# Opening of the first layer: four blocks per channel group, every modulation sum on VectorE, and a new order of transfers

## What is computed

```
mod = dot(silu(c), w_ada) + b_ada
shift, scale, gate = split(mod, 3)
u = rms_norm(x, norm_w) * (1.0 + scale) + shift
proj = dot(u, w_in)
(fq, fk, fv, ff, fg, dq, dk, dv, iq, ik, iw, dg, sz, sxbc, sdt, mg) = split(proj, split_points)
```

## Time and profile before

| | |
|---|---|
| median of three runs | 3430.95 us (3424.48 to 3431.2) |
| the profiled execution | 3426.33 us, its span 3424.5 us |
| mean granted TensorE clock | 0.986 of full speed |
| TensorE busy | 3300.5 us, 96% of the span |
| VectorE busy | 2245.1 us, 66% |
| ScalarE busy | 1699.9 us, 50% |
| GpSimd busy | 46.8 us, 1% |
| transfers | 719.31 MB, mean 210 GB/s |

### The profile page before, as it was taken

The page is one execution under the profiler, slowest core; times in us unless marked ns, Lnnn a source line. Parts: engine busy times, 40 slices in busy tenths (PEclk is TensorE's granted clock), DMA queues, the critical chain, the costliest instruction groups (busy, mean ns, idle before and its releaser), DMA issues.

```text
span 3424.5 us, 43659 instructions
## 1 busy us (share of the span) xinstructions
PE 3300.5 (96%) x18122; PEld 2865.5 (84%) x18122; DVE 2245.1 (66%) x2695; ACT 1699.9 (50%) x2096; POOL 46.8 (1%) x90
## 2 busy tenths in 40 slices
PE   4899999999999999999999999999999999999998
PEld 3689979788888887898898878888898899988887
DVE  6778877866666556786666576655567776544454
ACT  4355664654443445556646544444447865434343
POOL 0000000000000000000000000000000000000000
PEclk8899999999999999999999999999999999999999
DMA  9754566567777555444444567765555443465553
GB/s 376 286 213 174 187 240 255 210 239 267 261 266 296 204 196 184 172 159 169 172 179 160 175 244 272 271 234 197 186 185 192 178 172 134 163 221 192 190 190 140
DMA packets 102917, 719.31 MB, mean 210 GB/s; under 512 B 12176, under 2 KB 12256, under 8 KB 18752
## 3 DMA queue, kind: packets, MB, share of 16 engines
q1 hardware_dynamic: 93888, 675.38, 53.6%
q0 software_dynamic: 8256, 37.64, 3.1%
q10 hardware_dynamic: 576, 3.50, 0.3%
HBM read 710.08 MB, written 6.40 MB: 209 GB/s over the span
## 4 chain that ended last, share of the span: by engine, by line
PE 87%; DVE 8%; ACT 3%; issue 1%; DMA 1%; DVEq 0%; ACTq 0%
PE G L1258 80%; DVE LL L1862 3%; PE BA L1406 1%; PE BD L1379 1%; PE BD L1441 1%; DVE S L2070 1%; DVE RAW L1873 1%; DMA KV<-in_x_dram 0%; ACT HH L1501 0%; PE BC L1392 0%; DVE RAW L1855 0%; DMA RAW<-in_w_ada_packed_dram 0%; PE BE L1324 0%; PE BA L1460 0%; PE BC L1460 0%
## 5 line engine op out<-in xcount | busy, mean ns | idle before, releaser
L1501 ACT ACTIVATE HH<-RAW 128x2048 fp32r<-128x2048 f32 x546 | 1044.8, 1914 | 1091.5 <-PE G L1258 1063.9
L1862 DVE TENSOR_TENSOR LL<-RAW,HH 128x2048 fp32r<-128x2048 f32 x546 | 1247.7, 2287 | 357.0 <-ACT HH L1501 356.6
L1258 PE MATMUL G<-HH,UH 128*128 128x512 f32 x2528 | 1005.7, 398 | 45.4 <-DVE LL L1862 40.5
L1258 PE MATMUL G<-LL,UH 128*128 128x512 f32 x2528 | 989.4, 391 | 0.0
L1258 PE MATMUL G<-HH,UL 128*128 128x512 f32 x2528 | 989.1, 391 | 0.0
L1258 PE MATMUL G<-UH,HH 128*128 128x256 f32 x2080 | 603.7, 290 | 11.6 <-DVE XS L2106 7.7
L1258 PEld LDWEIGHTS G<-HH,UH 128*128 128x128 f32 x2528 | 477.8, 189 | 149.8 <-DVE LL L1862 47.4
L1258 PE MATMUL G<-UH,LL 128*128 128x256 f32 x2080 | 589.7, 283 | 0.0
L1258 PE MATMUL G<-UL,HH 128*128 128x256 f32 x2080 | 589.6, 283 | 0.0
L1258 PEld LDWEIGHTS G<-LL,UH 128*128 128x128 f32 x2528 | 477.3, 189 | 101.4
L1258 PEld LDWEIGHTS G<-HH,UL 128*128 128x128 f32 x2528 | 477.9, 189 | 99.2 <-issue 2.6
(11 more groups left out here) (360 smaller groups left out, 2309.4 us busy)
## 6 DMA issues: line engine op xcount, KB each, us to landing
RAW<-in_w_in_packed_dram SPq DMA_DIRECT2D x402, 1024.0 KB, 4.8
RAW<-w_ada_turned_packed_dram SPq DMA_DIRECT2D x92, 1024.0 KB, 4.9
RAW<-in_w_out_packed_dram SPq DMA_DIRECT2D x48, 1024.0 KB, 4.8
RAW<-in_w_o_ssd_packed_dram SPq DMA_DIRECT2D x32, 1024.0 KB, 4.8
RAW<-in_w_o_fox_packed_dram SPq DMA_DIRECT2D x16, 1024.0 KB, 4.8
RAW<-in_w_o_dsa_packed_dram SPq DMA_DIRECT2D x16, 1024.0 KB, 4.8
RAW<-in_w_proj_a_packed_dram SPq DMA_DIRECT2D x16, 1024.0 KB, 4.8
RAW<-in_w_proj_b_packed_dram SPq DMA_DIRECT2D x16, 1024.0 KB, 4.8
```

The costliest lines, as they stand in the source:

```text
L1258: mm = pe.matmul(to, lt, rh, start=first, stop=end, skip_group_check=True)
L1501: a.activation(HH[g % NH][:, :n], RAW[buf(ch["f"])][:, :n], ACT.Copy).then_inc(*hi_done.up(g))
L1862: v.tensor_tensor(LL[buf(f)][:, :n], RAW[buf(f)][:, :n], HH[g % NH][:, :n].bitcast(F32), ALU.subtract).then_inc(*lo_done.up(g))
```

## The change

All eight dots of a group are made on VectorE, and the TensorE version of a dot with its banks, its semaphore and its addition in `am_first` is gone. A fourth block, the first half of `dq`, begins in `open` with the others, so there are four chunks per group; it sums in banks BD and BE. The transfers get an order of their own: eight dots, then a chunk behind every second dot, and the last three chunks at the end. Dots use five buffers (6, 7, 8, 0, 1), chunks four (2 to 5). The products are emitted one at a time, behind the first, third, fifth and seventh dot of the next group, each `lo` right before its product and the next chunk's `hi` after it. The four blocks' heads are turned into the banks of their own block and no longer into BE and BD, and these blocks no longer give their banks free early (`free_by`). `ada_maybe` uses what was already fetched, also where nothing new is to be fetched. In the plan, `dq` after `misc` is one block (four chunks) in place of two.

```diff
-DOT_BUFS, CHUNK_BUFS = [6, 7, 8, 0], [1, 2, 3, 4, 5]
+DOT_BUFS, CHUNK_BUFS = [6, 7, 8, 0, 1], [2, 3, 4, 5]
...
-        b = {"n": n, "set": n if n < 3 else (n - 3) % 2, "x": x, "ready": ready, "kts": kts, "evac": evac, "chunks": chunks,
+        b = {"n": n, "set": n if n < 4 else n % 2, "x": x, "ready": ready, "kts": kts, "evac": evac, "chunks": chunks,
...
-        if a["every"] and a["i"] < len(a["list"]):
+        if a["got"]:
+            self.ada_chunk()
+        if a["every"]:
             a["count"] += 1
-            if a["got"]:
-                self.ada_chunk()
             if a["next"] < len(a["list"]) and a["count"] * a["every"][0] % a["every"][1] < a["every"][0]:
                 self.ada_fetch()
...
     def open(self, blocks, between, am, u):
...
+        def dot(gi, i):
+            return "scale" if i < 4 else "shift", 4 * gi + i % 4
+
+        parts = [b["chunks"][gi] for gi in range(4) for b in blocks]
...
+        for n in range(32):
+            kind, ct = dot(*divmod(n, 8))
+            src = ("w_ada_turned", 0, (D if kind == "scale" else 0) + ct * P, P, [(0, D)])
+            self.dots[kind, ct] = self.fetch(src, ("dot_dve", kind, ct))
+            if n >= 7 and n % 2:
+                bring()
+        while len(self.chunks) < len(parts):
+            bring()
+
+        def multiply(g):
+            self.put("lo", g)
+            if g % 4 < 3:
+                self.put("hi", g + 1)
+            self.gemm(parts[g])
+            self.slot()
 
         for gi in range(4):
-            dots = [("scale", m, "dve") for m in range(4)] + [("shift", m, "dve") for m in range(4 - ON_PE)]
-            for m in range(4 - ON_PE, 4):
-                dots.insert(6, ("shift", m, "pe"))
-            for i, (kind, m, engine) in enumerate(dots):
-                if 4 <= i < 7:
-                    self.bring(chunk(gi, i - 4))
-                self.dot(kind, 4 * gi + m, engine)
+            for i in range(8):
+                self.put("dot_dve", *dot(gi, i))
                 between(gi, i)
-                if gi and i == 1:
+                if gi and i == 0:
                     u(gi - 1)
-                    multiply(gi - 1, (0, 1))
-                elif gi and i == 3:
-                    multiply(gi - 1, (2,))
+                if gi and i % 2 == 0:
+                    multiply(4 * gi - 4 + i // 2)
+            self.put("hi", 4 * gi)
             am(gi)
         u(3)
-        for n in range(2):
-            self.put("lo", chunk(3, n)["g"])
-        self.gemm(chunk(3, 0))
+        for g in (12, 13):
+            self.put("lo", g)
+            self.put("hi", g + 1)
+        self.gemm(parts[12])
         self.slot()
-        self.pend += [chunk(3, 1), chunk(3, 2)]
+        self.put("lo", 14)
+        self.put("hi", 15)
+        self.gemm(parts[13])
+        self.slot()
+        self.pend += parts[14:]
...
-            o.blocks[b]["free_by"] = ("hd_scaled" if HEADS[h[0]][0] else "hd_copied", h, 1)
...
-            o.open(iq_b + [dkv_b], first_x, am_first, u_first)
+            dq_b = [o.wblock(w, DQ, heads(("dq", 0, 0), True), u_ready, kind="tm", begun=True)]
+            o.open(iq_b + [dkv_b] + dq_b, first_x, am_first, u_first)
...
-        dq_b = [o.wblock(w, DQ + j * 512, heads(("dq", l, j)), u_ready, kind="tm") for j in range(2)]
+            dq_b = [o.wblock(w, DQ, heads(("dq", l, 0)), u_ready, kind="tm")]
+        dq_b.append(o.wblock(w, DQ + 512, heads(("dq", l, 1)), u_ready, kind="tm"))
...
-    GB.append([BA, BC])
+    GB += [[BA, BC], [BD, BE]]
...
     def turn_bank(h, t):
-        return BD if t and h in o.two_banks else BE
+        return GB[o.blocks[o.head_block[h]]["set"]][t] if h in o.own_banks else BE
...
         def am_first(gi):
...
-            v.wait_ge(*dot_pe.at("shift", c + 3))
-            v.tensor_tensor(SH[:, e:c + 4], pe_part[:, e - c:4], MOD[:, e:c + 4], ALU.add).then_inc(*own.up())
+            v.tensor_tensor(SH[:, c:c + 4], DOT[:, 0, c:c + 4], MOD[:, c:c + 4], ALU.add).then_inc(*own.up())
```

More of the change, by code:

```diff
@@ L31 @@
 NR, NX, NH = 6, 3, 3
-ON_PE = 1
-DOT_BUFS, CHUNK_BUFS = [6, 7, 8, 0], [1, 2, 3, 4, 5]
+DOT_BUFS, CHUNK_BUFS = [6, 7, 8, 0, 1], [2, 3, 4, 5]
 HEADS = {"iq": (None, "idx", 4), "dk": ("dsa", "rot", 2), "dq": ("dsa", "rot", 4), "fq": ("fox", None, 4),
@@ L115, in __init__ @@
         self.packed = {}
-        dots = list(DOT_BUFS)
-        self.ring, self.buf_user = {"dot_dve": dots, "dot_pe": dots, "all": list(CHUNK_BUFS)}, {}
+        self.ring, self.buf_user = {"dot_dve": list(DOT_BUFS), "all": list(CHUNK_BUFS)}, {}
         self.fetches = []
@@ L124, in __init__ @@
         self.evac_before, self.side_before = {}, {}
-        self.user = [None, None, None]
+        self.user = [None] * 4
         self.ada = {"list": [], "i": 0, "job": None, "every": 0, "count": 0, "next": 0, "got": []}
@@ L308, in ada_all, with bring @@
         self.until(a["job"])
[L310 to L317, removed]
-    def open(self, blocks, between, am, u):
[L323 to L330, removed]
-        for gi in range(4):
-            dots = [("scale", m, "dve") for m in range(4)] + [("shift", m, "dve") for m in range(4 - ON_PE)]
-            for m in range(4 - ON_PE, 4):
-                dots.insert(6, ("shift", m, "pe"))
-            for i, (kind, m, engine) in enumerate(dots):
-                if 4 <= i < 7:
-                    self.bring(chunk(gi, i - 4))
-                self.dot(kind, 4 * gi + m, engine)
+    def open(self, blocks, between, am, u):
+        def dot(gi, i):
+            return "scale" if i < 4 else "shift", 4 * gi + i % 4
+        parts = [b["chunks"][gi] for gi in range(4) for b in blocks]
+        def bring():
+            ch = parts[len(self.chunks)]
+            ch["g"] = len(self.chunks)
+            self.chunks.append(ch)
+            ch["f"] = self.fetch(ch["src"], ("gemm_done", ch["g"]))
+        for n in range(32):
[12 more added lines that the diff above has]
+            self.slot()
+        for gi in range(4):
+            for i in range(8):
+                self.put("dot_dve", *dot(gi, i))
@@ L378, in rope, with heads @@
         side_ended("rope_sin", r, 1)
-    def heads(h, two_banks=False):
+    def heads(h, own_banks=False):
         def at_once(b):
             o.head_block[h] = b
-            o.two_banks.add(h)
+            o.own_banks.add(h)
             for t in range(2):
                 put("hd", h, t)
-            o.blocks[b]["free_by"] = ("hd_scaled" if HEADS[h[0]][0] else "hd_copied", h, 1)
             yield
@@ L392, in steps @@
         def steps(b):
-            if two_banks:
+            if own_banks:
                 yield from at_once(b)
@@ L557, in out_layer @@
                 o.evac.add(modulated(l + 1))
-    o.head_block, o.tok_block, o.freed, o.two_banks = {}, {}, {}, set()
+    o.head_block, o.tok_block, o.freed, o.own_banks = {}, {}, {}, set()
     def load_layer(which):
@@ L982, in hybrid_stack @@
     ld_fk = count("ld_fk", o.all("fk_load"), 16)
-    dot_pe, dot_dve = count("dot_pe", o.all("dot_pe")), count("dot_dve", o.all("dot_dve"))
+    dot_dve = count("dot_dve", o.all("dot_dve"))
     ld_cb, cb_tanh, cb_silu = count("ld_cb", [()], 16), count("cb_tanh", [()]), count("cb_silu", [()])
@@ L1265, in begin @@
             pe.wait_ge(*ld_cst.at())
[L1267 to L1276, removed]
         def gate_cols(l):
@@ L1321, in hd_turn @@
             pe.wait_ge(*(hd_rot if rot else hd_scaled).at(h, t))
-            pe.wait_ge(*(hd_put.at(h, 0) if t and h not in o.two_banks else evac_before("hd", h, 0)))
+            pe.wait_ge(*(hd_put.at(h, 0) if t and h not in o.own_banks else evac_before("hd", h, 0)))
             for c in range(n):
@@ L1462, in lru_pe @@
             mm.then_inc(*lru_mm.up(ct))
-        todo = {"gemm": gemm, "start": begin, "dot_pe": dot, "gate_cols": gate_cols, "x_in": x_in, "xn_pe": xn_pe,
+        todo = {"gemm": gemm, "start": begin, "gate_cols": gate_cols, "x_in": x_in, "xn_pe": xn_pe,
                 "m_turn": m_turn, "hd_turn": hd_turn, "misc_pe": misc_mm,
@@ L1942, in am_first @@
             c = 4 * gi
-            e = c + 4 - ON_PE
-            pe_part = (BD, BE)[gi % 2]
             v.wait_ge(*ld_mod.at())
             v.wait_ge(*ld_par[0].at())
-            v.wait_ge(*dot_dve.at("shift", e - 1))
+            v.wait_ge(*dot_dve.at("shift", c + 3))
             v.tensor_tensor(AM[:, c:c + 4], DOT[:, 0, 16 + c:20 + c], MOD[:, 16 + c:20 + c], ALU.add).then_inc(*own.up())
-            v.tensor_tensor(SH[:, c:e], DOT[:, 0, c:e], MOD[:, c:e], ALU.add).then_inc(*own.up())
-            v.wait_ge(*dot_pe.at("shift", c + 3))
-            v.tensor_tensor(SH[:, e:c + 4], pe_part[:, e - c:4], MOD[:, e:c + 4], ALU.add).then_inc(*own.up())
+            v.tensor_tensor(SH[:, c:c + 4], DOT[:, 0, c:c + 4], MOD[:, c:c + 4], ALU.add).then_inc(*own.up())
             v.wait_ge(*own.last())
```

## The result

The changed kernel takes 3412.66 us (median of five runs, 3411.43 to 3414.68), the kernel before 3430.76 us (median of five, 3424.48 to 3431.2): the ratio is 0.9953, with a 95% interval of 0.9939 to 0.9967. The forecast was 3403 us, with a range of 3394 to 3421. So the direction is right and the time lies in the range, but the profiled executions differ by only 3426.33 - 3413.68 = 12.65 us, where the sum of the prediction said 24.2. About half of the sum was lost again. The kernel before has executions of 3424 to 3428 us and others of 3430 to 3432 (31 and 19 of its 50), and its profile (3426.33) is of the first kind, which is why the profiles differ by less than the medians.

The account below looks back on a forecast made before the run. The prediction took the length of a group's loop to bound the opening, and TensorE everything after. 10.8 + 16.4 - 3 = 24.2 us off the profiled 3426.3 gave 3402, forecast as a median of 3403 us, range 3394 to 3421.

Parts of the forecast that it names:

- Term one: Opening: the last group's first product starts at 135.6 instead of 146.4 us, a gain of 10.8 us.
- the first rival: Opening: transfers keep today's share of 0.94, 2.65 us each, 6 us later; 3409 us, chance 0.12.
- Term two: Behind the opening: TensorE has three chunks less to do, at 5.48 us each, a gain of 16.4 us.
- Term three: Convolution: side work behind `misc` starts later and its heaviest steps meet convolution steps, a cost of 3 us.
- The clock: Opening: slow clock after idle time between single chunks, 8.0 us per chunk after a fall; counted as costing nothing.
- The third rival: Opening: TensorE stays at 1.2 GHz throughout, 10.2 us per chunk, ending at 169; about 3434 us, chance 0.07.
- The second rival: Convolution: side work's delay costs some 15 us, 0.6 in each of 24 chunks; 3415 us, chance 0.14.
- The fourth: Before 350 us: VectorE bounds the stretch and the gain is given back; no change, 3429 us, chance 0.07.

Follow-up runs that it names:

- the best kernel: Changed kernel with two steps of side work instead of one behind four chunks at the end of the convolution: 3407.26 us, ratio 0.9941.
- the early catching up: Changed kernel with the four missing side steps taken behind chunks 45, 48, 51 and 53: 3411.05 us, ratio 0.9953.

## Why the prediction was half right

**Term one, the opening: right.** 9.45 us for 10.8. Cycle, start and end were as worked out. The 1.3 us that are missing are a start 0.3 later, a cadence of 2.51 us for each transfer instead of 2.49, and what is left behind the last dots. VectorE keeps up, no buffer is asked for late (the experiment with other buffers changes nothing), and the first rival (0.94 share) is refuted by the windows. What made the gain is less the removal of TensorE's dots, to which the prediction gave its first place: it alone gives 5.7 of the 17.4 us that the opening gives with three blocks. That the rest is the new order is argued by elimination: other buffers make no difference, pairs of products 2.7 us, and no run has the new order alone.

**Term two, three chunks less: right.** 15.9 us for 16.4.

**Term three: this is the step that failed, in size and in place.** The prediction put it at 3 us, at the meeting of `misc`'s side work and the convolution. That meeting costs no more than it said, 1.6 us of idle time and clock by the end of the convolution: TensorE's waits from 140 to 350 us on `LL`, first row of the list of waits of the changed kernel,

```profile
PE G L1265 <- DVE LL L1858: 4.4, 6, 1.7
```

were 2.6 without the one of 6.6 at 146.4. Idle time by 400 us is 2.4 us more than before. But the prediction followed the late lane only to the end of the convolution. The lane stays late for some 70 chunks, and where it meets the evacuation of the `sz` blocks, full steps of the attention stand in place of empty ones. From chunk 89 to 92 that is 5.2 us, the largest single piece. The whole term measures 12.6 us where the sum has 3. From 400 to 760 us there are 4.0 us more idle (15.8 against 11.8), and the granted clock was at 0.50 for 6.8 us between 640 and 760 before, for 17.1 after. Both experiments on the lane bear this out: making the old kernel's lane late costs it 9.1 us, clear of the noise, and catching up gives back 6.7 us of the changed one's profiled span (5.4 in the medians, 4.1 in the ratios, which is within the intervals). How much of the 12.6 the lateness causes isn't measured to the microsecond. The lateness is four chunks, not the five of the prediction.

**The clock: counted as nothing, and rightly so in the opening.** The third rival (1.2 GHz throughout) did not come: 0.95 to 1.00 from 60 to 120 us. By the section HAM oscillation of the Trainium skill (TensorE: Matmul & The Clock Gate), tiles shorter than the wait for their data go back to the slow clock one after the other; here the chunks of 5.5 us were longer than the 0.9 to 3.5 us between them, and the trace shows no fall at every chunk, only one of 3.4 us between 60 and 120 us, behind an idle stretch of 3.48 us at 73.5. Such a fall costs nothing there, as the prediction argued: with other buffers the clock fell twice for 6.8 us, and the last group started at 136.96 all the same. But the term was not nothing later: 6.1 of the 12.6 us lost are clock. The prediction had seen in the earlier trace rows that an idle stretch of some 2 us can cost the clock or not, and asked it only of the opening. It should have been asked of every idle stretch that the change makes longer.

**The second rival** (side work's delay costs some 15 us) had the right source and nearly the right size, with the wrong place: it gave 3415, against the 3413.68 profiled. Its size is luck, since it charged 0.6 us to each convolution chunk, and up to their end 1.6 us in all are lost. The range held for the same reason: it reached as far as this rival. **The fourth** (given back before 350 us) is refuted by the same 1.6 us at chunk 45.

**What stays open.** That lateness of the lane costs time is shown, and so is what it does around `lo` of chunk 90. That the attention's rows make the waits there longer is read from four kernels, and no run changed the order of those instructions alone. The 1.6 us between chunks 45 and 89, the 2.6 between 92 and 110 and the 1.6 behind aren't traced to a cause. Part of the 2.6 isn't the lateness: at 717.95 TensorE waits 2.24 us where it waited 1.70 before, and it does so in the kernels that catch up too, while the kernel before with its lane late has 1.70. How the two lanes would have to meet so that neither the catching up nor the meeting costs anything was not found: the best kernel still idles 5.0 us more than the kernel before. And a lead read between chunks 45 and 100 holds side work that a kernel has not done yet; only after both lanes are empty (chunk 110: 13.9 in the changed kernel, 20.7 in the one caught up) does it compare like with like.

## What to carry to other kernels

A change that moves one lane of interleaved work against another must be priced wherever the two still run side by side, not only where it is made: follow the lane to its end, and look for places that already idle. When a bound engine loses its gain again, split its time into idle time, slow clock and work, because the clock can cost as much as the waits. And test a bundle by its parts: here the new order and VectorE's dots, without the fourth block, gave the same time as the whole change.

## What the runs showed of the hardware

Transfers of 1 MB from HBM ran at 420 to 423 GB/s for 100 us on end (20 to 120 us of the changed kernel), one landing every 2.51 us beside busy VectorE, ScalarE and TensorE. TensorE kept its clock of 1.00 from 100 to 120 us with 15.4 of 20 us busy and idle stretches of 3.22, 0.88 and 1.07 us between chunks.

The length of an idle stretch doesn't say what it costs in clock. 1.70 us at 228 left the clock at 1.00 in the changed kernel and was followed by 3.4 us at 0.50 in the early catching up, whose program is the same up to there. A stretch of 2.24 us near 688 was followed by 6.8 us at 0.50 in the changed kernel, where another of 0.68 us ends 0.7 us ahead of it, by 3.4 us in the one that catches up behind chunks 69 to 75, and by none in the other three that catch up. Two stretches of 2.41 and 2.84 us, 4 us apart, had each 3.4 us at 0.50 behind them in all three profiles that have them.
